# One layer of a diffusion backbone: order of the S5 matrices, the decayed keys, the last S5 products and one adaLN sum

## The reference, cut to what matters

```
m  = silu(c) @ ada_w + ada_b            # nine groups of 1024: shift, scale, gate of three sub-layers
x  = x + m2 * 0.5 * swiglu(mod(rms(x), m0, m1))       # first feed-forward, 1024 -> 2816 -> 1024, the context too
h  = mod(rms(x), m3, m4);  u,q,k,v,r,glr,ga,gb = split(h @ w_in)
ya = s5(u)      # diagonal complex SSM, two directions: B-bar = (lam_bar-1)/lam * B, scan, C; gelu; * sigmoid(y @ glu_w)
yb = gla(q,k,v,glr)   # chunked linear attention, two directions, gates by a low-rank map, k * exp(g_last - gc) etc.
x  = x + m5 * ((sigmoid(ga) * (ya @ s5_out) + sigmoid(gb) * (yb @ gla_out)) @ w_o)
x  = x + m8 * 0.5 * swiglu(mod(rms(x), m6, m7))       # second feed-forward, latents only
return rms(x)
```

## Time and profile before

| what | value |
|---|---|
| median of three runs | 1359.78 us (1358.69, 1359.78, 1369.3) |
| the profiled execution, own time | 1359.11 us |
| its span | 1357.4 us, 21462 instructions |
| PE busy | 1336.7 us (98%) |
| VectorE / ScalarE / GpSimd busy | 872.8 / 400.1 / 649.5 us |
| mean granted clock of TensorE | 0.997 |
| HBM | 156.93 MB read, 19.86 MB written |

### The profile page before, as it was taken

The page is one execution under the profiler, slowest core; times in us unless marked ns, Lnnn a source line. Parts: engine busy times, 40 slices in busy tenths (PEclk is TensorE's granted clock), DMA queues, the critical chain, the costliest instruction groups (busy, mean ns, idle before and its releaser), DMA issues.

```text
span 1357.4 us, 21462 instructions
## 1 busy us (share of the span) xinstructions
PE 1336.7 (98%) x8546; PEld 1231.0 (91%) x8546; DVE 872.8 (64%) x1376; ACT 400.1 (29%) x757; POOL 649.5 (48%) x408
## 2 busy tenths in 40 slices
PE   6999999999999999999999999999999999999998
PEld 4899999999999999998888888888998999999997
DVE  5885567667755755437656649926778665555666
ACT  4320010210210110124635321222132455545455
POOL 1644444443543543532732356637466456665554
PEclk9999999999999999999999999999999999999999
DMA  9553354353454334223322479584736233344322
GB/s 362 155 149 89 120 146 124 112 159 114 125 139 134 107 127 150 62 55 109 86 56 51 131 207 253 161 267 141 230 90 193 63 94 94 103 117 115 102 72 85
DMA packets 236782, 178.18 MB, mean 131 GB/s; under 512 B 33416, under 2 KB 211852, under 8 KB 236684
## 3 DMA queue, kind: packets, MB, share of 16 engines
q1 hardware_dynamic: 216624, 145.78, 37.4%
q10 hardware_dynamic: 20060, 31.04, 7.0%
HBM read 156.93 MB, written 19.86 MB: 130 GB/s over the span
## 4 chain that ended last, share of the span: by engine, by line
PE 92%; DVE 3%; DMA 2%; ACT 1%; SPq 1%; issue 1%; DVEq 0%; ACTq 0%
PE ps L1244 45%; PE ps L1566 14%; PE ps L1968 13%; PE ps L2027 7%; DMA ada_w<-in_ada_w_dram 2%; PE ps L1255 1%; PE ps L1843 1%; PE ps L2054 1%; PE ps L1880 1%; DVE ada_acc L2857 1%; PE ps L1669 1%; PE ps L1487 1%; PE ps L1438 1%; PE ps L1706 1%; PE ps L1679 0%
## 5 line engine op out<-in xcount | busy, mean ns | idle before, releaser
L1143 POOL TENSOR_SCALAR w_hi<-w_raw 128x1024 fp32r<-128x1024 f32 x128 | 154.3, 1205 | 532.3 <-PE ps L1244 276.5
L1146 POOL TENSOR_TENSOR w_lo<-w_raw,w_hi 128x1024 fp32r<-128x1024 f32 x128 | 322.9, 2523 | 10.7
L1244 PE MATMUL ps<-h_hi,w_lo 128*128 128x384 f32 (+2 forms) x1000 | 291.4, 351 | 0.0
L1244 PE MATMUL ps<-h_hi,w_hi 128*128 128x384 f32 (+2 forms) x1000 | 287.1, 346 | 0.0
L1244 PE MATMUL ps<-h_lo,w_hi 128*128 128x384 f32 (+2 forms) x1000 | 287.0, 346 | 0.0
L1244 PEld LDWEIGHTS ps<-h_hi,w_lo 128*128 128x128 f32 x1000 | 178.8, 188 | 15.0 <-issue 4.3
L1244 PEld LDWEIGHTS ps<-h_hi,w_hi 128*128 128x128 f32 x1000 | 180.4, 188 | 10.7
L1244 PEld LDWEIGHTS ps<-h_lo,w_hi 128*128 128x128 f32 x1000 | 180.6, 188 | 10.4
L1222 POOL TENSOR_TENSOR w_lo<-w_raw,w_hi 128x512 fp32r<-128x512 f32 x90 | 115.7, 1298 | 106.0 <-ACT w_hi L2606 104.5
L2857 DVE SCALAR_TENSOR_TENSOR ada_acc<-ada_w,cs,ada_acc 128x1024 f32<-128x1024 f32 x70 | 108.5, 1584 | 8.8 <-DMA ada_w<-in_ada_w_dram 6.7
L1968 PE MATMUL ps<-h_hi,w_hi 128*128 128x256 f32 x360 | 102.0, 283 | 0.0
(11 more groups left out here) (459 smaller groups left out, 2643.7 us busy)
## 6 DMA issues: line engine op xcount, KB each, us to landing
w_raw<-in_ffn_w_gate_dram SPq DMA_DIRECT2D x44, 512.0 KB, 4.9
w_raw<-in_ffn_w_up_dram SPq DMA_DIRECT2D x44, 512.0 KB, 4.1
w_raw<-in_ffn_w_down_dram SPq DMA_DIRECT2D x44, 512.0 KB, 4.1
ada_w<-in_ada_w_dram ACTq DMA_DIRECT2D x32, 512.0 KB, 3.8
w_raw<-in_w_in_dram SPq DMA_DIRECT2D x32, 512.0 KB, 4.2
ada_w<-in_ada_w_dram SPq DMA_DIRECT2D x30, 512.0 KB, 4.5
c_scr<-cp ACTq DMA_DIRECT2D x16, 288.0 KB, 3.6
b_scr<-bt_sb ACTq DMA_DIRECT2D x16, 256.0 KB, 3.6
```

The source lines that it names most:

```text
L1143: pool.tensor_scalar(w_hi[:, s, 0:cols], w_raw[:, s, 0:cols], 1.0, 1.0, ALU.mult, ALU.mult)\
L1146: pool.tensor_tensor(w_lo[:, s, 0:cols], w_raw[:, s, 0:cols], w_hi[:, s, 0:cols].bitcast(F32), ALU.subtract).then_inc(w_split, 1)
L1244: last = pe.matmul(mv[2], st, mv[part], start=(first and q == 0), stop=(n == len(terms) - 1 and q == 2))
```

## The change

Four edits. (1) `s5_input` and `s5_b(i, 0)` move from the head of side segment i + 1 to the end of the tiles of the segment before it, ahead of that segment's x updates. (2) `ke` is made first of the three and tells `e_d` by itself; `kz` tells it again; PE's `scores` and ScalarE wait for the second count. (3) The first `ma` product waits for the reading of glu slot k ahead of its part k, where all four waits stood ahead of it. (4) In the first segment of the second feed-forward the adds are moved: tile 3 of the last adaLN group is added at the end of hidden tile 0 in place of the beginning of hidden tile 1.

```diff
@@ PE
             def turn_keys(p):
-                pe.wait_ge(e_d, p + 1)
+                pe.wait_ge(e_d, 2 * p + 1)
...
             def scores(p):
                 j = GJ["sc", p]
+                pe.wait_ge(e_d, 2 * p + 2)
...
                 for k in range(4):
                     if ready:
-                        terms.append((ready, k + 1))
+                        terms.append(ready(k))
...
-            for c in range(4):
-                was_read(pe, MJ["glu", c])
+            def ya_read(k):
+                j = MJ["glu", k]
+                return slot_read[j % 4], j // 4 + 1
             for i in range(KD):
-                out_product("ma", i, JOB["ma"] + i, ya_hi, ya_lo)
+                out_product("ma", i, JOB["ma"] + i, ya_hi, ya_lo, None if i else ya_read)
@@ ACT
-                    act.wait_ge(e_d, p - 1)
+                    act.wait_ge(e_d, 2 * (p - 1))
@@ DVE, ffn
-                    s5_n[0] = 0
...
-                        if part.side and f_ == 0:
-                            s5_input(i)
-                            s5_b(i, 0)
...
-                            for k in range(*((0, 2), (3, 6), (7, 8), (8, 8))[f_]):
+                            for k in range(*((0, 2), (4, 6), (7, 8), (8, 8))[f_]):
                                 ada_add(ADA_MIX + 1, k)
                             tiles_of_h(f_)
-                            for k in ((2,), (6,), (), ())[f_]:
+                            for k in ((2, 3), (6,), (), ())[f_]:
                                 ada_add(ADA_MIX + 1, k)
...
+                    assert not part.side or s5_n[0] == S5_LINKS
+                    if q == 0 and nth < BATCHES:
+                        s5_n[0] = 0
+                        s5_input(nth)
+                        s5_b(nth, 0)
                     for k in range(KD):          # the x updates
@@ DVE, decayed
+                TT(ke[:, :], kt[:, ti, :], g_d[:, :], ALU.mult).then_inc(e_d, 1)
                 TT(e1q[:, :], qt[:, ti, :], g_a[p % 2][:, 0:NL], ALU.mult)
-                TT(kz[:, :], kt[:, ti, 0:NL], g_b[:, 0:NL], ALU.mult)
-                TT(ke[:, :], kt[:, ti, :], g_d[:, :], ALU.mult).then_inc(e_d, 1)
+                TT(kz[:, :], kt[:, ti, 0:NL], g_b[:, 0:NL], ALU.mult).then_inc(e_d, 1)
```

More of the change, by code:

```diff
@@ L1917, in _ @@
                 elif name == "mb":
-                    out_product("mb", i, MJ["mb", i], yb_hi, yb_lo, None if i else yb_ok)
+                    out_product("mb", i, MJ["mb", i], yb_hi, yb_lo, None if i else lambda k: (yb_ok, k + 1))
                 else:
-                    out_product("glu", i, MJ["glu", i], y_hi, y_lo, None if i else yl_ok)
-            for c in range(4):
-                was_read(pe, MJ["glu", c])
+                    out_product("glu", i, MJ["glu", i], y_hi, y_lo, None if i else lambda k: (yl_ok, k + 1))
+            def ya_read(k):
+                j = MJ["glu", k]
+                return slot_read[j % 4], j // 4 + 1
             for i in range(KD):
-                out_product("ma", i, JOB["ma"] + i, ya_hi, ya_lo)
+                out_product("ma", i, JOB["ma"] + i, ya_hi, ya_lo, None if i else ya_read)
             def out_job(q, j, c):
@@ L3260, in seg @@
                     read(js.down(KD - 1))
-                    assert not part.side or s5_n[0] == S5_LINKS
                 for part in parts:
```

## The result

In the first comparison the changed kernel took **1355.41 us** in the median (1354.47 to 1356.55, 13 executions), the kernel before 1359.51 (13 executions), and the ratio of the two came out as 0.9948, interval 0.9923 to 0.9973, that is 7.1 us, three times my forecast. That ratio says too much (the quotient of the medians is 0.9970). Five of the 13 executions of the kernel before lay at 1368.5 to 1370.4 us; in the three later comparisons, on other occasions, none of 80 executions of it was above 1361.5. This is the figure that I explain. I had forecast 1356.8, that is 2.3 us less than the profiled execution of the kernel before.

What follows compares the result with a forecast made beforehand. TensorE, busy 98% of the span, bounds the kernel, so only its pauses can be won: 0.92 + 0.54 + 0.59 + 0.29 = 2.34 us off 1359.11 gives 1356.8 us, range 1354.3 to 1360.2.

Steps and rivals of the forecast that it cites:

- the last load and add come about 2 us sooner: Last adaLN group: adding tile 3 earlier brings the last add to about 1037.5, before TensorE asks at 1039.25.
- term of 0.29: Last adaLN sums: TensorE's pause of 0.29 us ahead of them would go; lower bound 0.
- I found no wait on something that runs by its own clock in between.: Between the edited places everything follows TensorE, so a pause removed moves all behind it forward.
- Term 0.92: Turns of c_in in four side segments: a pause of 0.23 us each, 0.92 us won; bounds 0 and 1.4.
- the 0.3 us in segment 0: Moved S5 step of 4.75 us makes segment 0's x updates 0.3 us late, at no cost: 1.8 us to spare.
- 8.5 us for the step: Slower rival: the S5 step must take some 8.5 us in all four segments; about 1361.6 us, chance 0.06.
- GpSimd has nothing to split: At the S5 step's new place GpSimd waits for down products, so the step takes 4.75 us, upper end 6.9.
- Terms 0.54 + 0.59 = 1.13: Pauses at ke's turns for p = 2 (0.54 us) and the first ma product (0.59 us) both go.
- the case that it stays: Main case: the half-clock stretch behind the last adaLN sums remains, only the pauses are won; 1356.8 us, chance 0.42.
- R1: Rival: the clock also stays up behind the last adaLN sums; 4.0 us won in all, 1355.1 us, chance 0.25.
- R2: Rival: half the pauses return, only ke first and ya tile by tile pay; 1.13 us, 1358.0 us, chance 0.15.
- R3: Rival: nothing is seen, each pause becomes an equal one a little later; 1359.1 to 1359.8 us, chance 0.12.

Runs made afterwards that it cites:

- after: The profiled execution of the changed kernel with all four edits, from the first comparison: 1355.94 us, span 1354.2.
- e5: The changed kernel measured again with no further edit, beside the kernel before: 1355.09 us, ratio 0.9976.
- e1: The kernel before, unchanged, timed against itself: 1358.43 us, ratio 0.9999.
- e4: The kernel before with only the S5 matrices moved ahead of the x updates: 1358.09 us, ratio 0.9995.
- e11: The changed kernel with one product of the moved S5 step made five times: 1365.87 us, ratio 1.0056.
- e9: The kernel before with only ke made first and ya waited for tile by tile: 1358.21 us, ratio 0.9994.
- e2: The changed kernel without the moved adaLN add, its other three edits kept: 1355.35 us, ratio 0.9978.
- e3: The kernel before with only the add of the fourth adaLN tile moved: 1357.36 us, ratio 0.999.
- e7: The changed kernel with VectorE's last addition to the tiles of h behind the first x update, two rests one update later: 1354.81 us, ratio 0.9976.
- before: The profiled execution of the kernel before, from which the prediction was made: 1359.11 us, span 1357.4.
- e6: The changed kernel with the last adaLN sums put behind three matmuls of the first down product: 1355.88 us, ratio 0.9981.
- e8: The changed kernel with sums behind three down matmuls and the first x update ahead of the last h addition: 1354.75 us, ratio 0.9971.
- e10: The changed kernel with the last adaLN tile's add behind the tiles of h of hidden tile 2: 1362.1 us, ratio 1.0027.

## Why the prediction was half right

The forecast was 2.3 us. Edits 1 to 3 gave by the traces what their terms say, 2.2 for 2.05. The step that failed is edit 4: "the last load and add come about 2 us sooner". The last load is sent off at most 0.4 us sooner and the last add starts no sooner; what the edit changes is whether GpSimd is at work when that add starts. Its term of 0.29 measured 0.35 to 1.17 us beside a kernel with the same other edits. In a second thing the forecast had nothing at all: one of the three times before lay at 1369.3 us, I called it scatter, and five of 13 such executions made the first ratio three times my forecast.

**What bounds.** Right that TensorE's pauses set the time, and that they can be read from starts. Wrong in one sentence: "I found no wait on something that runs by its own clock in between." From the last adaLN add to the first x update VectorE has 12.5 us of work with hardly any idle time (1037.75 to 1050.24 after; 1036.19 to 1048.69 in e5; 1040.06 to 1052.55 in e1), and TensorE waits at both ends of it. This chain was there before, and I could read only its first end, because in that one execution the half clock hid the second.

**Edit 1.** Term 0.92, measured 0.96 (e4) to 1.04. The step's length, the 0.3 us in segment 0 and the idle c_in all as forecast. The price of failure was not: I had the kernel fall behind the one before only at 8.5 us for the step. Run e11 made it nominally 7.6 us, lost 10.8 against e5 and is some 7 us slower than before. "GpSimd has nothing to split" holds at the new place only up to 0.7 us behind the end of the step in segment 0 (126.25, GpSimd 126.98).

The Trainium skill says in the GPSIMD Engine Reference, section 1 (Specifications), that GpSimd contends with VectorE's instructions that have two SBUF inputs. The traces agree at both places: 1.44 us for a product of 0.71, and 1.85 to 3.2 for the last add, alone 1.28. Which of the two waits is seen in e5: the one that starts second.

**Edits 2 and 3.** Terms 0.54 + 0.59 = 1.13, measured 0.54 + 0.60 by the gaps and 1.24 to 1.30 over the stretch. No exposed weight load at the three waits: at most 0.24 us from each matmul to the next in the first ma product. What I did not see is that 0.3 us of it comes back at the last sums as long as edit 4 is not there (e9, and e2 with edit 1 as well: 0.51 to 0.82).

**Edit 4.** The first half came true: the load of tile 5 is sooner. The step that failed is the next one: "the last load and add come about 2 us sooner: at about 1037.5, while TensorE asks at 1039.25". Add 5, started 1.4 to 1.5 us sooner (e3, e5, after), took 3.2 to 3.4 us for 2.1 to 2.3, because GpSimd subtracts beside it and it ends 1.08 us behind that subtraction in every one of the 13 profiles. So it ends at most 0.4 us sooner, and with it the last load is sent off. And the last add would not have come much sooner with its tile there: VectorE comes to the add only behind `act_lo` of hidden tile 2, and that follows TensorE. The add starts 1.39 to 1.79 us ahead of the last up matmul without edit 4 and 1.15 to 1.50 with it (after, e3, e5, e7, e11), so not sooner at all. The wait for the tile was no property of the kernel either (0.59 us in before, 0.34 in e4, none in e1, e2 and e9; 0.2 of each stands ahead of the add in any case). I also added a start and a duration as if the duration were fixed. For the last add it is 1.28 us if GpSimd starts nothing before it (e3, e5, e6, e7, e8) and 1.85 to 2.55 if GpSimd is at work by then (before, after, e1, e2, e4, e9). In the first case the 0.29 us are won and some of the second pause with them.

From the seventh sums to the first group product the traces have 84.04 us in e1 and 83.58 in e3, which differ by edit 4 alone; 84.55 in e2 and, with edit 4 added, 83.38 in e5 and 84.20 in after. The stretch repeats within 0.03 us where only edit 1 differs (84.01 in e4, 84.54 in e9). So edit 4 is worth 0.45, 1.17 and 0.35 us there, though the pause ahead of the sums is 0.15 longer in after than in the kernel before. It pays by these five executions, not through the wait for the tile that I had costed, but by moving GpSimd's work out of the add's way. The medians can't show it: e2 and e5 differ by 0.26 us.

**The clock.** I took the fall as a fact of the kernel before and of its sums, with 0.42 for the case that it stays and 0.25 that it goes. It is neither: with a pause of 0.26 to 0.59 us ahead of the same sums it fell in one profile of six (before; not in e1, e2, e4, e9, after) and without a pause in none of six, which tells nothing of so short a pause; with one of 3.65 it had fallen when the sums began. So part of the 4.0 us that I gave R1 was a difference between executions and not between kernels; comparing profiles without the fall (e1 and e5, loading phase taken off) 2.9 us are left, of which 2.25 lie up to the seventh sums and 0.66 behind them. The rest up to the medians' 3.4 lies within the intervals. The mean clocks of the executions don't help here, because a fall can lie elsewhere. Five of the 13 profiles have one in the loading phase (before, after, e4, e7, e9). That of e4, whose mean is 0.997, shows a granted clock of 0.50 from 27 to 33 us and 1.00 from 1042 to 1046. Its fall lasts 6.8 us, in e7 and e9 it lies at 43 to 47 us, and these are the three whose first gate matmul starts behind 59.5 us; all others lie at 57.67 to 58.72. So the scatter of the loading phase and the falls in it go together; which brings the other is not shown.

The Trainium skill, TensorE: Matmul & The Clock Gate, Part 1, says that how many matmuls run slow at the start of a kernel varies from run to run. Here it was so in the middle of one, before against e1. Had I carried that over to the earlier trace rows, one row of one execution would not have carried a term.

**R2 and R3** fell: all of edits 1 to 3 is seen. The sum that the traces bear out is 0.96 + 1.24 for them, and behind the seventh sums -0.15 (after) to 0.66 (e5) for edit 4 less what edits 2 and 3 give back there, with no term for the clock.

## What to carry to other kernels

How long a VectorE instruction takes depends on what GpSimd is doing when it starts; before adding one to a start, lay GpSimd's timeline over it, at the new place and for as long as the step could slip. Before costing a sooner load, ask what else the instruction stands behind: here its own engine's order held it. When one pause is taken away, look for the other end of the chain it belongs to: shortening the wait ahead of the sums alone moved it to the fifth down product. And a stretch at half clock in a single profile is no term of a sum until a second execution shows it; it can also hide the wait that you will meet next.

## What the runs showed of the hardware

- An add of 1.28 us that begins while GpSimd subtracts ends 1.08 to 1.09 us after that subtraction, whenever it began: the add of tile 5 in all 13 traces (2.1 to 3.45 us long), the last add in six (before, e1, e2, e4, e9, e10); behind a GpSimd copy it was 1.07 (after). One that begins first takes 1.28 us even if GpSimd begins beside it, and then it is GpSimd's instruction that is longer (2.05 us for 1.04, e5).
- 2.85 us more of VectorE work in each of four segments cost 10.8 us in all, where the room that I had read would have left 1.7: in segment 0 it grew by 3.6 us through contention (5.75 for 2.87, 1.41 for 0.69), and the pause of 5.35 us there was followed by 5.5 us at 1.2 GHz.
- One kernel, on one occasion, had 5 of 13 executions 10 us longer than the rest, with 80 later ones showing none. What it was these runs do not tell.
